# Other shapes for the products of ones ahead of the first tile, in a hybrid decoder step on one core

## The reference

```python
h = rmsnorm(x, norm1_w)
proj = h @ w_in                      # (592 x 2048) @ (2048 x 8208)
# gated DeltaNet, 8 heads: causal conv on q/k/v, triangular solve per chunk of 64
# HGRN2, 8 heads: chunked form with decay per channel
x = x + concat(gdn_out, hgrn2_out) @ w_out
u = relu(rmsnorm(x, norm2_w) @ w_up)
x = x + (u * u) @ w_down
return rmsnorm(x, final_norm_w), new states
```

## Time and profile before

| | |
|---|---|
| median of three runs | 2925.43 us |
| lowest and highest | 2922.65 and 2929.58 us |
| span of the profiled execution | 2921.5 us, granted clock 0.998 in the mean |
| TensorE busy | 2888.7 us (99%) |
| VectorE, ScalarE, GpSimd busy | 2048.1, 1147.6, 319.2 us |

### The profile page before, as it was taken

How to read it: one execution, slowest core, us unless ns; L and a number is a source line. 1 busy time by engine, 2 the same in 40 slices (tenths; PEclk the granted TensorE clock), 3 DMA queues, 4 the chain that set the end, 5 groups by cost and what they waited for, 6 DMA issues and landing times.

```text
span 2921.5 us, 51592 instructions
## 1 busy us (share of the span) xinstructions
PE 2888.7 (99%) x21560; PEld 2842.0 (97%) x21560; DVE 2048.1 (70%) x2865; ACT 1147.6 (39%) x1440; POOL 319.2 (11%) x472
## 2 busy tenths in 40 slices
PE   9999999999999999999999999999999999999998
PEld 8999999999999999999999999999998999999998
DVE  6666665657575757565587777777778878887885
ACT  4333333333333323334354444444434444444454
POOL 5201111110101020102100000000000000000111
PEclk9999999999999999999999999999999999999999
DMA  7344783333334533345344554554476666666665
GB/s 210 68 93 71 87 77 82 78 87 79 84 80 79 80 72 89 101 129 156 96 135 147 154 151 136 157 154 141 138 250 213 193 193 199 188 193 201 195 190 203
DMA packets 516475, 396.51 MB, mean 136 GB/s; under 512 B 18930, under 2 KB 484196, under 8 KB 516244
## 3 DMA queue, kind: packets, MB, share of 16 engines
q1 hardware_dynamic: 462272, 267.95, 39.0%
q0 software_dynamic: 22672, 88.35, 8.3%
q10 hardware_dynamic: 31300, 36.93, 4.0%
HBM read 308.80 MB, written 84.37 MB: 135 GB/s over the span
## 4 chain that ended last, share of the span: by engine, by line
PE 85%; DVE 5%; issue 5%; DMA 1%; ACT 1%; POOL 1%; SPq 0%; DVEq 0%; POOLq 0%; ACTq 0%
PE main L1360 40%; PE main L993 26%; PE mx L1360 7%; PE mx L1244 2%; PE mx L1150 1%; PE mx L1141 1%; PE mx L1065 1%; DVE w_lo L1960 1%; POOL sq_sum L910 1%; PE mx L1081 1%; PE mx L1124 1%; PE mx L1185 0%; PE mx L1251 0%; DVE w_lo L2561 0%; DMA u_forms<-ub 0%
## 5 line engine op out<-in xcount | busy, mean ns | idle before, releaser
L993 PE MATMUL main<-h_hi,w_hi 128*128 128x296 f32 (+1 forms) x2592 | 607.5, 316 | 5.9 <-DVE h_lo L1972 2.2
L1360 PE MATMUL main<-forms_a,w_hi 128*128 128x288 f32 x3024 | 606.2, 296 | 4.8 <-DVE w_lo L2561 4.5
L1360 PE MATMUL main<-forms_b,w_hi 128*128 128x288 f32 x3024 | 603.8, 295 | 0.5 <-DVE w_lo L2561 0.5
L993 PE MATMUL main<-h_lo,w_hi 128*128 128x296 f32 (+1 forms) x2592 | 563.0, 299 | 0.0
L993 PE MATMUL main<-h_hi,w_lo 128*128 128x296 f32 (+1 forms) x2592 | 562.1, 298 | 0.0
L1360 PEld LDWEIGHTS main<-forms_a,w_hi 128*128 128x128 f32 x3024 | 487.2, 189 | 6.9 <-DVE w_lo L2561 6.9
L1360 PEld LDWEIGHTS main<-forms_b,w_hi 128*128 128x128 f32 x3024 | 484.5, 188 | 0.7 <-DVE w_lo L2561 0.7
L1360 PE MATMUL main<-forms_a,w_lo 128*128 128x288 f32 x1512 | 448.0, 296 | 0.0
L1360 PE MATMUL main<-forms_b,w_lo 128*128 128x288 f32 x1512 | 445.1, 294 | 0.0
L993 PEld LDWEIGHTS main<-h_hi,w_hi 128*128 128x128 f32 x2592 | 414.1, 190 | 19.2 <-issue 8.7
L993 PEld LDWEIGHTS main<-h_hi,w_lo 128*128 128x128 f32 x2592 | 420.2, 189 | 0.0
(11 more groups left out here) (402 smaller groups left out, 3575.7 us busy)
## 6 DMA issues: line engine op xcount, KB each, us to landing
w_raw<-in_w_in SPq DMA_DIRECT2D x128, 512.0 KB, 7.7
w_raw<-in_w_up SPq DMA_DIRECT2D x128, 512.0 KB, 5.0
w_raw<-in_w_down SPq DMA_DIRECT2D x100, 512.0 KB, 6.4
u_forms<-ub POOLq DMA_DIRECT2D x32, 1152.0 KB, 6.2
z<-x_scratch SPq DMA_DIRECT2D x32, 576.0 KB, 6.5
x_scratch<-z POOLq DMA_DIRECT2D x31, 576.0 KB, 6.6
stage<-u_forms ACTq DMA_DIRECT2D x30, 576.0 KB, 3.9
w_raw<-in_w_out SPq DMA_DIRECT2D x32, 512.0 KB, 4.0
```

What stands on the lines that cost most here:

```text
L993: ins = mm(out[:, half, :], w[:, ring, k, :], x[:, kx, half * width:half * width + width], start=first and n == 0, stop=last_ and n == 2)
L1360: ins = mm(out, w[:, k, :], x[:, kx, :], start=i in (0, 1, 3) and k == 0 and n == 0, stop=k == KP - 1 and n == 2, skip_group_check=True)
```

## The change

`warm(WARM)` at the head of TensorE's stream goes. In its place stand 40 fp32r products (the matrix of ones as weights, a piece of it repeated four times as the moving operand) and 112 fp32 products that use only a part of the array: 64x64, 32x32, 128x32, 32x128 or 128x64 rows by columns of weights, with 16, 32, 64 or 128 moving columns, in one place of the array or in two or four places in turn. They write to `main` and `mx`, both overwritten later. The two later calls (`WARM_AT`) and all other engines stay as they are.

```diff
-            warm(WARM)
+            def warm_wide(n, width):
+                one = ones[:, :].bitcast(F32R)
+                part_ = width // 4
+                wide = one[:, 0:part_].unsqueeze(1).to_broadcast([P, 4, part_])
+                for i in range(n):
+                    mm(main[i % 2][:, 0, 0:width].rearrange("p (a n) -> p a n", a=4), one, wide, start=True, stop=True)
+
+            def warm_tiles(n, rows, cols_, width, places):
+                for i in range(n):
+                    r, c, bank_ = places[i % len(places)]
+                    mm(mx[c:c + cols_, bank_, 0:width], ones[r:r + rows, 0:cols_], ones[r:r + rows, 0:width],
+                       start=True, stop=True)
+
+            warm_wide(16, 512)
+            warm_wide(12, 336)
+            warm_wide(12, 256)
+            warm_tiles(12, 64, 64, 32, [(0, 0, 0), (64, 64, 1)])
+            warm_tiles(12, 64, 64, 32, [(0, 0, 0)])
+            warm_tiles(16, 32, 32, 16, [(0, 0, 0), (32, 32, 1), (64, 64, 2), (96, 96, 3)])
+            warm_tiles(16, P, 32, 16, [(0, 0, 0), (0, 32, 1), (0, 64, 2), (0, 96, 3)])
+            warm_tiles(16, 32, P, P, [(0, 0, 0), (32, 0, 1), (64, 0, 2), (96, 0, 3)])
+            warm_tiles(16, P, 32, P, [(0, 0, 0), (0, 32, 0), (0, 64, 0), (0, 96, 0)])
+            warm_tiles(12, 64, 64, P, [(0, 0, 0), (64, 64, 1)])
+            warm_tiles(12, P, 64, 64, [(0, 0, 0), (0, 64, 1)])
             pe.wait_ge(s_mask, 5)
```

## The result

The changed kernel takes 2938.56 us in the median of six runs (2934.90 to 2940.99), the one before 2926.30 us in the median of six beside it. The ratio is 1.0042, with a 95% interval of 1.0030 to 1.0055: slower by 12.3 us, 8.8 to 16. The forecast was 2945.3 us with a range from 2936 to 2957, so the direction and the range held, and the size of the delay was put at 19.9 us instead of 12.3.

What follows compares the result with a forecast made beforehand. TensorE, busy 2888.7 of 2921.5 us, was taken to bound the kernel. Wide products to 10.8 us plus 18.5 us of tiles start the turns at 29.3, 19.9 late: 2925.4 + 19.9 = 2945.3 us, range 2936 to 2957.

Steps and rivals of the forecast that it cites:

- The start of the turns sets the end, one for one: Head of TensorE's stream: turning the first token blocks D later moves everything behind by D; forecast 19.9 us.
- D: Delay of the start of the turns on TensorE against 9.4 us before; forecast 29.3 - 9.4 = 19.9 us.
- The rival of the other side: Between the turns and 64.88 us: the start isn't on the path, the delay is taken up; 2928 us, chance 5%.
- The distance to the factor: VectorE, from its first copy of `xT` to its copy of the norm's factor: 38.3 us, unchanged within 2 us.
- The wide products: Head of TensorE's stream: the 40 fp32r products end at 10.8 us, bounds 8.2 and 13.8.
- The tiles, 18.5 us: Behind the wide products: 112 part-array products, 224 records, take 6.7 + 9.8 + 2.0 = 18.5 us, bounds 10.1 and 25.0.
- the sign of a wrong price: Start of the turns outside 25 to 34 us would show the price of the tiles to be wrong.
- the first rival: Part-array products: places run side by side, D = 10.5 us, time 2935.9, up to about 2940; chance 17%.
- the rival's bound: Tiles with 128 moving columns, if places overlap: weight loads bound them at 0.060 us a record, 5.3 instead of 9.8 us.
- The changes of shape: Between the eight tile groups: a skill page says switching tiling mode drains TensorE, without a time; nothing was counted.
- The clock in the small tiles: Part-array products: clock falls to 0.50 from about 14 us, D = 37, 2962 us; milder form 2950; chance 18%.
- My argument against this rival: Near the kernel's end: 30 one-column products, 3.3 us in a row, left the clock at 1.00.

Runs made afterwards that it cites:

- e9: Kernel before the change with 14 instead of 18 products of ones ahead of the first tile: 2925.28 against 2925.57 us, ratio 0.9999.
- e11: Kernel before the change with SyncE's later loads held until the first block is turned: 2924.35 against 2925.57 us, ratio 0.9998.
- e6: Changed kernel with SyncE's loads from the third token quarter on held until the first block is turned, a single run: 2931.64 us.
- e4: Changed kernel with half as many products in each of the eight groups on part of the array: 2932.88 us, ratio 1.0025 to the kernel before.
- e10: Changed kernel with SyncE's later loads held until the first block is turned, six runs: median 2934.12 us, ratio 1.0030 to the kernel before.
- e2: Changed kernel with each group of part-array products kept in its first place: 2950.81 us, ratio 1.0086 to the kernel before.
- e7: Changed kernel without the 40 wide products, the 112 on part of the array kept, a single run: 2932.97 us.
- e8: Changed kernel with no products ahead of the first tile, the 7 and 11 later ones kept: 2926.65 against 2925.31 us, ratio 1.0000.

## Why the prediction was right, and where it was off

*The start of the turns sets the end, one for one.* Right. Over nine kernels the factor moves from -3.1 to +22.1 us and the time from -0.6 to +25.2. The times lie 0 to 4 us above the factor's shift in all but the changed kernel. The intervals are about 3 us to each side, so I read no second cost from this; and an offset of this sign is what the late factor in the profiled execution of before gives (48.46 us, against 45.3 in e9 and e11). The start at 9.41 us, from which the prediction measured D, was that of one late execution. The rival of the other side (5%) fell: nothing between the turns and the norm took up the delay. The distance to the factor, which the prediction wanted within 2 us of 38.3, was 36.7 to 38.8 us in all thirteen traces.

*The wide products.* 10.8 us predicted, 10.51 measured (9.8 to 10.9 in the other kernels, as the clock rises sooner or later).

*The tiles, 18.5 us.* This is the term that was mis-sized. Without the stop they took 7.4 us (e6), below my lower bound of 10.1; in the changed kernel 22.10 - 10.51 = 11.6. The turns began at 22.10 us, outside the 25 to 34 that the prediction had named as the sign of a wrong price. All three parts of the sum were too high: the narrow tiles took 3.1 us and not 6.7, those with 128 columns 3.8 (e6) and not 9.8, those with 64 columns 0.9 (e6) and not 2.0 (busy times of the groups, which overlap a little). I had priced the wide-moving tiles in changing places at the full array's 0.111 us a record, and that they run beside each other was the first rival (17%). The four-place groups gave 0.034 to 0.038. For the rival's bound I had taken 0.060, as if each weight load needed that long; the narrow groups at 0.013 show that loads for other places overlap as well. The Trainium skill's 3.07 for four row tiles of 512 columns ("TensorE: Matmul & The Clock Gate", section "Measured speedup vs the span model"), cited in the prediction, agrees with 0.111/0.036 = 3.1 for 128 columns here.

*The changes of shape*, at which the sum had nothing, do cost a little. Half of the records took 14.01 - 9.82 = 4.19 us (e4) and all of them 17.44 - 10.06 = 7.38 (e6). Twice the half is 1.0 us more than the whole, so by this estimate some 0.12 us at each of the eight groups doesn't shrink with the records. In e6's trace the first record of a new shape starts 0.11 to 0.20 us behind the last of the old one, while records of one group follow in 0.009 to 0.055 us. This agrees with the drain at a change of the tiling mode of the Trainium skill's page "TensorEngine Tiling (Array Packing)", section "Key Properties", cited in the prediction; no run tells the mode from any other change of shape.

*What was in nobody's account* is the wait for instructions: 2.92 us, and about 1.8 us more, mostly for the last records and the first transposes at 1.2 GHz behind it. From the first tile to the 7 products behind block 1 it is 23.67 - 10.51 = 13.16 us, in e6 without the stop 18.52 - 10.06 = 8.46, so 4.7 us in all.

That the range held is luck, then. The shorter tiles and this stop partly cancel. Without the stop the delay would by estimate have been 12.3 - 4.7 = 7.6 us, less than the range's lower end of 10.6, and e10 with most of the stop gone measured 2934.12 us, below 2936. The time that was measured also lies among those of the first rival (2935.9 to 2940) and not near the 2945.3 of the forecast.

*The clock in the small tiles* (18%). In the changed kernel it did not fall in them but behind the stop. In one place (e2) it did, for 10 us with TensorE busy all along, and one-column products went through such a fall at the end of the changed kernel's trace. My argument against this rival, that 30 of them had left the clock at 1.00, rested on one execution, and eleven of the thirteen traces are the other way.

## What to carry to other kernels

Filler ahead of the first real product is free only up to the moment at which the data arrives; behind it each microsecond is paid in full when TensorE bounds the kernel. Small products in changing places of the array run side by side, so price them by the place and not by the record, add some 0.1 us for each change of shape, and then check whether the instruction stream can keep up. Read a fall of the clock and a late start off more than one trace before you subtract two of them: one execution of the kernel before was 3.1 us late at the norm. When an engine idles with no releaser named, count its instructions up to the stop and look at the instruction queue: the same count in another order of work tells a refill from a cost of the instruction.

## What the runs showed of the hardware

- TensorE stopped behind 223 products' records (each with a weight load) in four kernels, for 0.66 to 2.92 us, and went on 2.6 to 2.9 us after the first packet on its instruction queue. Products at 0.11 us a record never met it. The packet itself took 1.1 us in the changed kernel, with and without held loads. What asks for it stays open. It came at 10.0 us in e7, at 12.0 and 14.5 in the changed kernel with held loads, between 15.75 and 17.5 in eight kernels, and at 23 to 24 in e8 and e9, with from 87 to 223 records of products started, so it goes neither by the time nor by the count.
- fp32 products in four places: 0.013 us a record for 16 columns (0.038 in one place), 0.036 for 128. A change of shape adds about 0.1 us.
- The clock fell to 0.50 in stretches without idle time: behind tiles of 16 columns in one place (e2, at 15 us), where it stayed down through the 32x128 tiles, and in the one-column products near the end in eleven of thirteen traces (at 2917.7 us in the changed kernel). There it came back during the transposes of line 1451, which were all that TensorE did from 2918.9 us on (0.50 up to 2924, 1.00 from 2926).
- From 1 to about 7 us the clock column shows 1.00 while products run at half their later pace. Paces, not the column, tell the clock ahead of the first event.
